# RWKV mixer: what the gates' block and the start of the recurrence do, and in which block they do it

## The reference, cut to what matters

```python
r, k, v, wd, ad, gd = jnp.split(p_rw, RWKV_SPLITS, axis=-1)
kk = heads(k * k_k)
kk = kk / jnp.maximum(jnp.sqrt(jnp.sum(kk * kk, axis=-1, keepdims=True)), 1e-12)
g = jax.nn.sigmoid(gd) @ g_up
for d in range(N_DIR):
    wlog = -jax.nn.softplus(-(w0[d] + jnp.tanh(wd[:, :, d]) @ w_up[d])) - 0.5
    decay = jnp.exp(-jnp.exp(wlog.astype(f32)))
    a = jax.nn.sigmoid(a0[d] + ad[:, :, d] @ a_up[d])
    kd = heads(k * (1 + (a - 1) * k_a))
    o = o + wkv7_scan(rh, heads(decay), kd, vh, kk, heads(a), reverse=(d == 1))
    bonus = bonus + jnp.sum(rh * kd * r_k.astype(f32), axis=-1, keepdims=True) * vh
```

## Time and profile before

| what | value |
|---|---|
| device time, median of 3 runs | 3275.98 us (3274.2 to 3276.07) |
| profiled execution, first to last instruction (span) | 3265.5 us |
| device time of the profiled execution by itself | not listed; the median is 10.5 us over this span |
| gates' block (first to last instruction) | 133.62 to 175.50 us |
| recurrence, first instruction to its first 64x64 matrix product (L1518) | 175.78 to 188.46 us |
| mean granted TensorE clock | 0.979 of 2.4 GHz |
| busy share of the span | PE 94%, DVE 70%, POOL 35%, ACT 30% |

### The profile page before, as it was taken

The page is one execution under the profiler, slowest core; times in us unless marked ns, Lnnn a source line. Parts: engine busy times, 40 slices in busy tenths (PEclk is TensorE's granted clock), DMA queues, the critical chain, the costliest instruction groups (busy, mean ns, idle before and its releaser), DMA issues. The chain is left out here.

```text
span 3265.5 us, 56686 instructions
## 1 busy us (share of the span) xinstructions
PE 3070.1 (94%) x20623; PEld 2697.4 (83%) x20623; DVE 2279.6 (70%) x4051; ACT 970.4 (30%) x1785; POOL 1128.0 (35%) x782
## 2 busy tenths in 40 slices
PE   8979979889999999999999999889998999799989
PEld 6568857789999999999999987668886777578867
DVE  7677676679898898588888875576773326567731
ACT  2334421233433333333333332542210023311200
POOL 5232224222122122153333334134554432445543
PEclk9989989999999999999999999999999999999999
DMA  4000022277877877799999943022223220222323
GB/s 161 26 2 3 3 78 81 87 238 240 279 254 251 274 246 256 262 379 346 356 339 352 346 136 113 7 71 95 95 77 89 83 63 30 62 94 96 106 62 97
DMA packets 214340, 508.99 MB, mean 156 GB/s; under 512 B 18534, under 2 KB 102646, under 8 KB 210588
## 3 DMA queue, kind: packets, MB, share of 16 engines
q1 hardware_dynamic: 155420, 322.15, 29.3%
q0 software_dynamic: 36864, 134.23, 12.6%
q10 hardware_dynamic: 21888, 50.34, 4.0%
HBM read 454.21 MB, written 52.44 MB: 155 GB/s over the span
## 5 line engine op out<-in xcount | busy, mean ns | idle before, releaser
L188 PE MATMUL ev_acc<-ev_w_high,ev_high 128*128 128x384 f32 x1024 | 343.0, 335 | 9.3 <-DVE ev_w_low L2599 9.3
L189 PE MATMUL ev_acc<-ev_w_low,ev_high 128*128 128x384 f32 x1024 | 342.8, 335 | 0.0
L190 PE MATMUL ev_acc<-ev_w_high,ev_low 128*128 128x384 f32 x1024 | 342.8, 335 | 0.0
L2549 POOL DMA_INDIRECT ev_rows<-in_v,ev_list x128 | 177.6, 1387 | 329.0 <-DVE ev_row_sum L2604 317.7
L188 PE MATMUL up_ps<-ffn_high,up_high 128*128 128x512 f32 x704 | 276.8, 393 | 5.5 <-DVEq L667 5.5
L190 PE MATMUL up_ps<-ffn_high,up_low 128*128 128x512 f32 x704 | 275.6, 392 | 0.0
L189 PE MATMUL up_ps<-ffn_low,up_high 128*128 128x512 f32 x704 | 275.5, 391 | 0.0
L183 POOL TENSOR_TENSOR up_low<-normed,up_high 128x1024 fp32r<-128x1024 f32 x88 | 211.3, 2402 | 178.1 <-DVE up_high L178 178.1
L188 PE MATMUL eu_ps<-norm_unit_high,eu_high 128*128 128x384 f32 x768 | 265.0, 345 | 0.0
L190 PE MATMUL eu_ps<-norm_unit_high,eu_low 128*128 128x384 f32 x768 | 257.2, 335 | 0.0
L189 PE MATMUL eu_ps<-norm_unit_low,eu_high 128*128 128x384 f32 x768 | 256.9, 335 | 0.0
(11 more groups left out here) (645 smaller groups left out, 7967.3 us busy)
## 6 DMA issues: line engine op xcount, KB each, us to landing
normed<-in_u SPq DMA_DIRECT2D x128, 512.0 KB
mixed<-in_v SPq DMA_DIRECT2D x128, 512.0 KB, 5.5
normed<-in_w_up SPq DMA_DIRECT2D x88, 512.0 KB, 3.4
expert_act<-mixed ACTq DMA_DIRECT2D x128, 192.0 KB, 4.3
expert_gates<-eu_gates ACTq DMA_DIRECT2D x24, 1024.0 KB, 6.9
expert_scores<-expert_gates SPq DMA_DIRECT2D x16, 1536.0 KB, 11.7
ev_act<-expert_act SPq DMA_DIRECT2D x128, 192.0 KB, 5.6
in_w_raw<-in_w_in SPq DMA_DIRECT2D x20, 512.0 KB, 3.4
```

The lines of the kernel that those rows point to most:

```text
L188: nc.tensor.matmul(out, w_high.bitcast(F32R), x_high.bitcast(F32R), start=start, stop=False)
L189: nc.tensor.matmul(out, w_high.bitcast(F32R), x_low.bitcast(F32R), start=False, stop=False)
L190: return nc.tensor.matmul(out, w_low.bitcast(F32R), x_high.bitcast(F32R), start=False, stop=stop)
L2549: nc.gpsimd.indirect_dma_start(rows[:, b % 4, :], None, v, bass.IndirectOffsetOnAxis(ap=list_[:, b % 8:b % 8 + 1], axis=0)).then_inc(fetch ...
```

## The change

What it does:

- The three weight matrices are loaded by SP at the end of `mixer_in`, into free tiles of `c.y`, and the tanh is taken there by ACT, after the 18th of 20 tiles, with the sigmoid table loaded behind it.
- `lw` is no longer multiplied by `-EXP_MINUS_HALF`. The four exponentials of each unit take it as their scale instead. POOL's eight multiplications in the gates' block are gone.
- In the gates' block PE makes the first four products for `a` before the key lengths, `lw`'s products before `gate`'s. ACT squares `k * k_k` from `p_t` with a scale, makes the first factor of `kd` for the second direction (an Identity with scale and bias), takes `lw` before the root and squares the root for DVE. DVE drops the four multiplications `kk = k * k_k` ahead of the lengths and one 128x1024 multiplication per half of the root; instead it makes `kk` in each half by two 128x512 operations.
- The new class `ScanAhead` holds the recurrence's constants and the preparation of a unit. POOL makes the constants in the gates' block, and unit (0, 0) is prepared in that block by DVE, ACT and POOL. `mixer_scan` starts at the front of that unit.

The diff, cut to its core:

```diff
@@ mixer_in
+                sp.wait_ge(late.summed, 1)
+                for place, source in ups:
+                    sp.dma_start(place, source).then_inc(ups_loaded, 16)
+                sp.wait_ge(ups_loaded, len(ups) * 16)
...
+                    if j == order.index(T_WD) + 1:
+                        act.wait_ge(shifted, j)
+                        nc.scalar.activation(tanh_w, p_t[:, T_WD, :], ACT.Tanh)
+                        nc.scalar.preload_act_table(ACT.Sigmoid)
@@ mixer_gates, ACT
+                square(0)
+                for n in range(first_decay):
+                    act.wait_ge(product, n + 1)
+                    nc.scalar.activation(a[:, n, :], ps[:, n % 4, :], ACT.Sigmoid, bias=col(c, "a0", n)).then_inc(drained, 1)
+                    if n + 1 < RT:
+                        square(n + 1)
+                    if n >= RT:
+                        act.wait_ge(less_made, 1)
+                        act.wait_ge(drained, n + 1)
+                        nc.scalar.activation(kd[:, n, :], a[:, n, :], ACT.Identity, scale=col(c, "k_a", n - RT),
+                                             bias=less_k_a[:, n - RT:n - RT + 1]).then_inc(damped_ahead, 1)
+                for n in range(first_decay, first_gate):
+                    act.wait_ge(product, n + 1)
+                    nc.scalar.activation(lw[:, n - first_decay, :], ps[:, n % 4, :], ACT.Sigmoid, bias=col(c, "w0", n - first_decay)).then_inc(drained, 1)
+                    if n == first_decay:
+                        for x in range(2):
+                            nc.scalar.activation(low[:, x, :], p_t[:, T_GD + x, :], ACT.Sigmoid).then_inc(low_ready, 1)
+                nc.scalar.preload_act_table_set("natural_log_exp_and_others")
+                root(0)
+                for at in ((1, 1), (2, 0), (2, 1)):
+                    ahead.prepare_act(act, 0, 0, at)
+                root(1)
+                for n in range(first_gate, tiles):
+                    act.wait_ge(product, n + 1)
+                    nc.scalar.activation(gate[:, n - first_gate, :], ps[:, n % 4, :], ACT.Copy).then_inc(drained, 1)
+                for at in ((4, 0), (4, 1)):
+                    ahead.prepare_act(act, 0, 0, at)
@@ mixer_gates, POOL
-                for n in range(2 * RT):
-                    pool.wait_ge(drained, first_decay + n + 1)
-                    pool.sem_inc(decay_met, 1)
-                    nc.gpsimd.tensor_scalar(lw[:, n, :], lw[:, n, :], -EXP_MINUS_HALF, None, ALU.mult).then_inc(decay_scaled, 1)
+                ahead.constants(pool)
+                pool.wait_ge(key_made, 1)
+                pool.wait_ge(key_rooted, 1)
+                ahead.prepare_pool(pool, 0, 0)
@@ mixer_gates, PE
+                for n in range(RT):
+                    tile(n)
+                for m in range(RT):
+                    length_of(m)
+                for n in range(RT, tiles):
+                    tile(n)
@@ mixer_gates, DVE
+                    t = half(sq, n)
+                    dve.wait_ge(rooted, 3 * n + 3)
+                    nc.vector.scalar_tensor_tensor(out=t, in0=half(length, n), scalar=-0.5, in1=t, op0=ALU.mult, op1=ALU.mult).then_inc(stepped, 1)
+                    for m in (2 * n, 2 * n + 1):
+                        nc.vector.scalar_tensor_tensor(out=kk[:, m, :], in0=p_t[:, T_K + m, :], scalar=col(c, "k_k", m), in1=inv[:, m, :],
+                                                       op0=ALU.mult, op1=ALU.mult).then_inc(stepped, 1)
+                    dve.wait_ge(stepped, 3 * n + 3)
+                    nc.vector.scalar_tensor_tensor(out=half(kk, n), in0=t, scalar=1.5, in1=half(kk, n), op0=ALU.add, op1=ALU.mult).then_inc(key_rooted, 1)
...
+                for at in ((0, 1), (1, 0), (1, 1)):
+                    ahead.prepare_dve(dve, 0, 0, at)
+                refine(0)
+                dve.wait_ge(key_rooted, 1)
+                ahead.prepare_dve(dve, 0, 0, (3, 1))
+                for m in range(RT):
+                    dve.wait_ge(pair_summed, m + 1)
+                    nc.vector.tensor_tensor(bonus[:, m, :], pb[:, m, :], p_t[:, T_V + m, :], ALU.mult).then_inc(bonus_made, 1)
+                refine(1)
@@ the exponentials of a unit
-                        act_s[d].ends(nc.scalar.activation(q[d], gt, ACT.Exp), "eq")
+            act_s.ends(nc.scalar.activation(self.q[d], gt, ACT.Exp, scale=-EXP_MINUS_HALF), "eq")
@@ mixer_scan
-                nc.scalar.preload_act_table_set("natural_log_exp_and_others")
-                for at in ((1, 1), (2, 0), (2, 1), (4, 0), (4, 1)):
-                    prepare(0, 0, at)
...
-                for at in ((0, 1), (1, 0), (1, 1), (3, 1)):
-                    prepare(0, 0, at)
```

377 lines of the change are left out of this document (184 added, 193 removed).

## The result

The changed kernel is slower: 3283.36 us median (3279.74 to 3290.9, 12 runs) against 3275.98 us (3274.2 to 3277.88, 12 runs), a ratio of 1.0028 with the interval [1.002, 1.0036]. The forecast was 3264.4 us, 3261.5 to 3269.0.

A forecast was written before the change was run, and what follows sets the result against it. It took chained waits between engines in the gates' block and recurrence start as the limit; savings of 2.7 us in the block and 8.9 at the start, 11.6 together, took 3275.98 to 3264.4 us, range 3261.5 to 3269.0.

The forecast's parts named there:

- the clock: Start of the gates' block: PE begins at the low clock and gets full clock after 5.1 us, at 138.9.
- bounds of 0 and 7.6 us: Gates' block: full clock at once or only after 7.6 us, moving the end by -2.6 or +1.2 us.
- the second rival: Gates' block: PE starts at full speed, saving 2.6 us more, 3261.8 us; chance 0.07.
- The last rival: Gates' block: PE stays at low clock throughout, net +12.4 us, 3288.4 us; chance 0.02.
- the prediction's own signs of being wrong: Among them, in the gates' block: ACT's L1092 ending after 163, or a table load followed by over 0.1 us idle.
- Input stage: ACT's table loads and tanh fit its idle time, weight loads queue behind SP's last load; cost 0.
- ACT: Gates' block: four sigmoid-Identity pairs at 1.36 us, further sigmoids, a table load to 157.0, then the root by 160.3.
- DVE: Gates' block: done with running sum and centring at 156.9, then waits 3.4 us for ACT's root.
- Recurrence's start: From block end to first matrix product: 3.8 us instead of 12.68, 8.9 us saved.
- The Identities: Gates' block: with the four back on DVE, the end would come 1.3 us earlier, with no other sign.
- What follows starts after the recurrence's barrier and shifts with it: Stages after the recurrence: they move with its earlier start; no size of their own.
- the 10.5 us to the median: Whole kernel before: median 3275.98 us lies 10.5 us over the profiled span of 3265.5 us.

The follow-up runs named there:

- run 12: Run 10's kernel plus six unread PE products behind tiles 5 to 10 of the gates' block; 3255.69 us.
- run 8: Changed kernel with Identities back on DVE, POOL's wait, unread PE products in the later stage and at both ends of the gates' block; 3251.73 us.
- run 10: Changed kernel with its four Identities left on ACT, plus run 8's unread PE products and POOL's wait; 3265.09 us.
- run 4: Changed kernel with the four Identities taken off ACT, DVE making all `kd` factors as before the change; 3266.36 us.
- run 6: Changed kernel with POOL waiting for DVE's `gla_k_past` in the gated linear attention's last head; 3276.82 us.
- run 5: Changed kernel with five unread products on PE behind tiles 12 to 16 of the gates' block; 3280.82 us.
- run 3: Changed kernel with six unread products on PE behind gates' products 5 to 10, where it waits for ACT; 3273.97 us.

## Why the prediction was wrong

The step that failed is the clock. "I take the clock back after the same 5.1 us, at 138.9", with bounds of 0 and 7.6 us, priced one rise and no further fall. PE began at full speed, as the second rival had it (first sigmoid at 134.94), the clock was low from 135.5 to 142.3, and that much moved the block little (the four other profiles of this mixer have the low clock at PE's start already, so the full one was a draw): ACT took product 4 at 145.55 where 144.3 was forecast. Then it fell a second time, at 152.6, for which the sum had no term. The last rival, "PE stays at the low clock through the whole block", named the mechanism ("its first products now come with gaps, since ACT spends 1.36 us per product of 0.86") and got 0.02, because the low stretches seen so far had ended 5.1 and 7.6 us behind PE's start. That was the wrong inference: the row of 5.1 us had PE fed without a gap by products over 128 rows; the new stretch has three waits ahead of it and lasts 27.3 us. Why it lasts so long stays open. The rival's price was too high (block end 196.8, by its own terms 196.5; measured 185.7), since the fall comes in the middle of the block. One of the prediction's own signs of being wrong came: ACT's L1092 ended at 164.58, behind 163.

Together: where the sum had the first product 11.9 us earlier, it came 1.1 us later.

The other terms, each against the changed profile:

- *Input stage*: cost 0, PE's first product at 133.81 (forecast 133.75). Right.
- *ACT*: the Identity costs 0.81, not 0.72, the pair 1.48, not 1.36: 0.5 us in four. The table load took 1.28 and Ln followed at once: right. The 2.66 us of the Trainium skill ("ScalarE: Activation LUTs", "What ACT_TABLE_LOAD costs"), a load of about 1.28 us and a drain, again doesn't hold as a whole: the load has that length, the drain isn't there. The first root came at 161.34 instead of 157.0, mostly because ACT's last sigmoids waited for PE at the low clock (one every 1.70 us).
- *DVE*: scan block to 158.4, the halves' operations at 1.22 and 1.23 without POOL beside them: right. The wait for ACT's root was there, 6.21 and not 3.4 us. `f` took 0.15, not the 1.22 of the earlier trace rows, where POOL worked beside it. Unforeseen was the wait of 8.16 us for PE's sums: PE was taken as done at 166.6 and ended at 181.2.
- *Recurrence's start*: block end to first product 3.9 us, forecast 3.8. Right. With the clock held, in run 12, the block ends at 173.95, forecast 172.8, and the product comes at 176.1, forecast 176.6. That is near in part by luck: run 12 has the full clock from the block's start, which the sum gave only as a favourable bound of 2.6 us.
- *The Identities*: the sum gave them 1.3 us "but no other sign". They cost 13.4 (runs 8, 10), and the sign hung on them: run 4 without them is faster than both kernels. The Trainium skill's rule ("ScalarE: Activation LUTs", "Rules for kernel authors": multiply and add on VectorE) stood against the change and was right. The reason that it gives, the cost per element, is not what decided here; run 12 shows 9.4 of the 13.4 us in PE's clock.
- *"What follows starts after the recurrence's barrier and shifts with it"*: wrong. A stage 2500 us later took 127.4 instead of 116.2 and 122.0 us. `gla_k_past` took 2.09 us in both full profiles of before and 5.6 in all of the changed kernel and its variants without POOL's wait. That DVE waits there for POOL, and that it costs some 5 us of the stage, is shown by run 6. Why the turn goes one way in one kernel and the other way in the other, with starts equal to 0.01 us, is open.

Two sizes of the frame were wrong too: one profiled execution was taken as typical, though the later stage varies by 6 us in before itself, and the 10.5 us to the median was treated as time around the span.

## What to carry to other kernels

Before moving work onto an engine that drains TensorE's products, compare its time per product with TensorE's: where it is longer, the price can be a half-speed TensorE for the rest of the block, here some 9 us for four operations of 0.8. A gain made in one block also shows only if the stages after it keep their own clock and their own turns; a few unread products in TensorE's waits, with POOL's wait, make such kernels comparable (before's runs then lie within 2.1 us, without them within 9.5) and were here worth 6.7 us to the kernel before by themselves. Of the kernels run, the fastest is run 8, the change with `kd` left on DVE, POOL's wait, and TensorE kept at work through its waits: 3251.73 us, 0.7% below before.

## What the runs showed of the hardware

- A low clock can outlast full work: PE worked without a gap from 152.2 to 181.2 us and the clock came back only at 179.9. In run 10 it lasted 27.3 us as well and ended at 177.1, 5.1 us behind the start of the four sums. In run 5, with unread products among the others, it lasted 13.7. PE's work in the low stretch included products over 128 rows from 159.2 us on; what ends it isn't known.
- Three waits of 0.36 us in a row, each before a product of 1.12 us, stood ahead of its fall from the full clock, in the changed kernel and in run 10. Runs 3 and 12 have none there and run 4 a single one of 0.49 us, and the clock doesn't fall. The Trainium skill says the like: "TensorE: Matmul & The Clock Gate", "A second HAM failure mode: psum-queue depth-cycling", tells of a kernel whose frequent short idle times between groups of products made the clock oscillate.
- An operation of DVE with two SBUF inputs took 0.67 us alone (`gla_k_future`, of the same form), 0.85 behind one of POOL's (run 6), 2.09 behind two and 5.62 behind four: held up whole, not slowed in proportion. The Trainium skill ("SBUF — State Buffer", "SBUF: two separate sides") describes an exclusive lock between such an operation and one of POOL's, which goes to whichever starts first, for the whole instruction. The trace agrees that one blocks the other; but DVE's operation, already waiting, was passed over by three further instructions of POOL in one kernel and by one in the other.
